# Output projections that open a group get no share of the selection and attention steps in the plan

## The reference

```python
q, k, v, qi, ki, wi, u = mixer_inputs(x, pos, g_pre, w_in)
# per block of 128 queries: index scores, the best 256 keys of each query, attention over these keys
idx = top_k(sum_h(relu(qi_h @ ki.T) * wi_h), 256)
a_o = sparse_attend(q, k[idx], v[idx])
s_o = glu_out(s5_scan(u), w_glu, b_glu)
x   = x + rmsnorm(concatenate([a_o, s_o]) @ w_out)        # output projection
hdn = square(relu(rmsnorm(x) @ w_up))                      # 1024 -> 4096
y   = x + rmsnorm(hdn @ w_down)                            # 4096 -> 1024
```

## Time and profile before

| | us |
|---|---|
| median of 3 runs | 3634.23 (3627.40 to 3640.02) |
| the profiled execution | 3627.5 |
| its span | 3625.8 |
| PE busy in the span | 3036.5 (84%) |
| DVE busy | 1840.4 (51%) |
| ACT busy | 1637.7 (45%) |
| POOL busy | 1262.6 (35%) |

### The profile page before, as it was taken

How to read it: one execution, slowest core, us unless ns; L and a number is a source line. 1 busy time by engine, 2 the same in 40 slices (tenths; PEclk the granted TensorE clock), 3 DMA queues, 4 the chain that set the end, 5 groups by cost and what they waited for, 6 DMA issues and landing times.

```text
span 3625.8 us, 46903 instructions
## 1 busy us (share of the span) xinstructions
PE 3036.5 (84%) x15347; PEld 2396.8 (66%) x15352; DVE 1840.4 (51%) x4116; ACT 1637.7 (45%) x2873; POOL 1262.6 (35%) x1181
## 2 busy tenths in 40 slices
PE   7998545546678889997799999968989999699997
PEld 5887431224556668764577886645778888588885
DVE  4433872862357884468686332666782333511112
ACT  3322413612447755575463555745634554322222
POOL 1333621324013561153265113522672112224444
PEclk9999777877879999998899999988999999899999
DMA  4444344636336564354454223343444213544443
GB/s 149 142 146 142 93 126 133 170 118 202 111 123 232 206 244 134 115 200 154 157 193 169 79 85 124 126 171 122 177 159 136 73 62 131 191 147 150 174 151 125
DMA packets 216109, 529.45 MB, mean 146 GB/s; under 512 B 57514, under 2 KB 110828, under 8 KB 189852
## 3 DMA queue, kind: packets, MB, share of 16 engines
q1 hardware_dynamic: 202924, 501.94, 40.6%
q0 software_dynamic: 11360, 22.60, 2.0%
q10 hardware_dynamic: 1584, 1.90, 0.2%
HBM read 399.43 MB, written 134.12 MB: 147 GB/s over the span
## 4 chain that ended last, share of the span: by engine, by line
PE 50%; DVE 11%; issue 9%; ACT 5%; DMA 4%; POOL 4%; SPq 2%; ACTq 0%; POOLq 0%; DVEq 0%
PE r L1620 16%; PE r L1657 12%; PE po L1708 6%; PE tr L1699 3%; ACT junk_a_b L1982 2%; PE sc L1686 2%; PE sc L1687 2%; POOL acc_b L2124 1%; PE sc L1676 1%; DVE junk_v_b L2363 1%; PE r L1817 1%; POOL hr_b L2105 1%; DVE trial_b L2315 1%; PE tr L1676 1%; PE r L1586 1%
## 5 line engine op out<-in xcount | busy, mean ns | idle before, releaser
L2124 POOL TENSOR_TENSOR acc_b<-acc_b,part_b 128x512 f32<-128x512 f32 x375 | 516.2, 1398 | 483.0 <-ACT part_b L1933 482.1
L1657 PE MATMUL r<-ready_b,h_b 128*128 128x512 f32 x2304 | 574.4, 403 | 41.5 <-ACT part_b L1933 38.3
L1657 PEld LDWEIGHTS r<-ready_b,h_b 128*128 128x128 f32 x2304 | 434.2, 193 | 155.5 <-ACT part_b L1933 51.1
L1620 PE MATMUL r<-x_hi_b,ready_b 128*128 128x512 f32 x1536 | 516.5, 400 | 5.4 <-DVE x_lo_b L2229 2.8
L2105 POOL TENSOR_TENSOR hr_b<-hr_b 128x512 f32<-128x512 f32 x128 | 149.0, 1164 | 766.7 <-ACT hr_b L1920 766.5
L1982 ACT ACTIVATE junk_a_b<-score_b,trial_b 128x384 int8<-128x384 f32 (+13 forms) x266 | 347.4, 1306 | 100.8 <-DVE trial_b L2315 99.7
L1620 PEld LDWEIGHTS r<-x_hi_b,ready_b 128*128 128x128 f32 x1536 | 291.3, 190 | 72.2 <-issue 10.1
L1933 ACT ACTIVATE part_b<-r 128x512 f32<-128x512 f32 x390 | 223.9, 595 | 220.5 <-PE r L1657 131.8
L1708 PEld LDWEIGHTS po<-V_sb,pT_b 128*128 128x128 f32 x2176 | 286.7, 191 | 23.4 <-ACT pT_b L2009 4.5
L1620 PE MATMUL r<-x_lo_b,ready_b 128*128 128x512 f32 x768 | 301.6, 393 | 0.0
L1708 PE MATMUL po<-V_sb,pT_b 128*128 128x64 f32 x2176 | 279.2, 268 | 3.7 <-DVE o_b L2380 3.3
(11 more groups left out here) (407 smaller groups left out, 6061.1 us busy)
## 6 DMA issues: line engine op xcount, KB each, us to landing
ready_b<-ws_u SPq DMA_DIRECT2D x96, 1024.0 KB, 6.6
ready_b<-ws_d SPq DMA_DIRECT2D x96, 1024.0 KB, 5.0
ws_u<-up_b SPq DMA_DIRECT2D x32, 1024.0 KB, 8.7
ws_d<-dn_b SPq DMA_DIRECT2D x30, 1024.0 KB, 6.4
kv_b<-kv_pages POOLq DMA_DIRECT2D x128, 128.0 KB, 3.5
kv_b<-kv_pages SPq DMA_DIRECT2D x128, 128.0 KB, 3.1
raw_b<-w_out SPq DMA_DIRECT2D x64, 256.0 KB, 3.2
raw_b<-w_up SPq DMA_DIRECT2D x32, 512.0 KB, 5.4
```

Of the source, the lines that this page charges most:

```text
L1620: mm = pe.matmul(x[:], wt[:, c], y[:, k], start=k == n == 0, stop=(k, n) == (KD - 1, 2))
L1657: mm = pe.matmul(x[:], f[:, tok], w[:, col], start=c == n == 0, stop=(c, n) == (KQ - 1, 2))
L2124: pool.tensor_tensor(dst, dst, part[:, add_no[key] % 2, :], ALU.add).then_inc(add_pool, 1)
```

## The change

The opening units W(g,0,i) count nothing in the plan, so `merge` puts no side steps behind them, and those steps are dealt over the U and D units. Nothing else is changed; the cost of a unit is read by `merge` alone. Every instruction of both kernels is the same but for what follows from the plan's order.

```diff
     def feed_units(g):
         T = nt(g)
-        out = [(("W", g, 0, i), 5.4) for i in range(T)]
+        out = [(("W", g, 0, i), 0.0) for i in range(T)]
```

## The result

The median went from 3631.35 us (3623.85 to 3640.02, 6 runs) to 3652.41 us (3648.27 to 3656.70, 6 runs): ratio 1.0057, 95% interval 1.0042 to 1.0071. The change makes the kernel 0.57% slower. The forecast was 2.8 us less (3631) and was wrong in its sign: the kernel got 21 us slower. The time lies outside the forecast's own range (3621 to 3645) and inside the wide one (3610 to 3656). The profiled execution took 3651.81 us.

What follows compares the result with a forecast made beforehand. PE, busy 84%, was taken as the bound, with only its holes to gain or lose. Openings -32.5 and moved steps +29.7 gave -2.8 us, so 3634.2 became 3631.4, rounded to 3631; own range 3621 to 3645, wide 3610 to 3656.

Steps and rivals of the forecast that it cites:

- Openings: Openings of groups 0 to 2 without side steps: 17.5, 8.3 and 6.7 us shorter, together -32.5 us.
- S(1,0) and the first of S(1,1) in U(0,0) and U(0,1): Selection steps moved out of group 0's opening: their index matmuls hold PE, costing 7.7 us.
- AB(1)'s cover: Wait for queries at attention's start after group 0: one U replaces four D as cover; cost 0 to 5.5, 3 taken.
- The price of a moved step: Selection stretches: each moved step costs the stretch's mean excess over its feed, 0.77, 0.49 and 0.81 us in groups 0 to 2.
- one choice that costs 5.9: Group 2: all six moved steps belong to one choice; a block beside a choice takes 29.30 us, without 23.40: 5.9 us.
- The rest: 0: Attention, three more D with `beside_search`, and the last attention step one D later: each costs 0.
- one step more in U(1,30) to D(1,15,3): End of group 1: these units get one more selection step, costing 2.3 us.
- DVE bounds group 0: Slower rival: DVE limits group 0's U and D, 15 steps at 3.04 us each; +17.3 us, 3651, chance 0.18.
- a block of 37 us or more beside S(1,2): Group 0's test: such a block, 34.20 us before, at 34 to 35 supports the forecast; 37 or more speaks for DVE.
- The stretch to AB(1): Group 0, from U(0,0): some 297 us if the forecast is right, 316 if DVE binds, 292 if steps hide.
- The port rule: DVE and POOL block each other at a shared SBUF port: ten moved steps lose 2.8 us if DVE is the bound.

Runs made afterwards that it cites:

- e1: Plan of before, with only the opening steps of groups 0, 1 and 2 dealt over their own group's U and D up to AB(g+1): 3651.69 us, 1.0057.
- e4: Plan of before, with only group 2's opening steps dealt over its U and D up to AB(3): 3629.99 us, 0.9994.
- e2: Plan of before, with only group 0's 15 opening steps dealt over its U and D up to AB(1): 3642.20 us, 1.0028.
- e18: The changed kernel with the hidden block's square made by ACT instead of POOL: 3615.83 us, 0.9957 against before.
- e3: Plan of before, with only group 1's 8 opening steps dealt over its U and D up to AB(2): 3645.72 us, 1.0041.
- e14: Plan costs of before, with all side steps 5 cost units (two to three steps) later against the feed: 3646.18 us, 1.0052.
- e5: Kernel of before with each choice's scan and following comparison covering only the first 128 columns, so work is left out: 3612.73 us, 0.9951.
- e13: Plan costs of before, with all side steps 3 cost units (one to two steps) earlier against the feed: 3638.40 us, 1.0017.
- e16: Plan costs of the changed kernel, with all side steps 8 cost units (about four steps) later: 3688.36 us, 1.0160 against before.
- e17: Kernel of before with the hidden block's square made by ACT instead of POOL: 3624.72 us, 0.9977.

## Why the prediction was wrong

- **Openings.** Right: up to U(g,0) they gave 38.2 us, where the sum had 32.5 up to W(g,1,0). Group 0's 26.6 us up to W(0,1,0) came to the tenth, U(0,0) at 1058.2 (about 1060 forecast), and the waits for the third tile's features stayed (11.31 and 8.72 us). The first halves gave 31.1 us of the 32.5 forecast for them; the second halves got 1.8 to 2.8 us shorter in each group, 7.1 in all, which the sum left out.
- **S(1,0) and the first of S(1,1) in U(0,0) and U(0,1).** Forecast 7.7 us, these two units grew by 6.9. Right.
- **AB(1)'s cover.** Bounds 0 to 5.5, value taken 3. PE's timeline shows 12.05 us where the earlier trace rows has 6.10, 5.95 us more: all of the lost cover (5.45) and 0.5 besides. The upper bound was the one to take, since only one U stood between the last selection step and the first attention step.

```profile
1370.49 0.79 PE L1686 MATMUL sc<-KS_sb,qh_b 128*128 128x512 f32 x1 [12.05 <-DMA ql_b<-ql_d]
```

- **The price of a moved step: the step of the sum that failed.** I took the mean excess of a stretch, 0.77, 0.49 and 0.81 us per step, as the price of one step more. But the excess is not made by steps evenly. In the later part of a selection (from U(1,6) and U(2,8) on) blocks without a choice take 21.8 to 24.4 us in before and after with six to eight steps, and one more costs next to nothing; those with three or more steps of a choice take 24.7 to 32.9, by where it falls; those with one or two take anything from 21.8 to 30.1. A denser plan moves every choice of its group against the blocks, and each falls anew. The forecast priced 6.9 + 3.9 us for the moved steps in groups 0 and 1 and 5.9 in group 2, 16.7 in all; the selection stretches took 44.0 less 6.9, 37 us. e1 shows that it is the moved steps that cost this; why they do is shown for U(2,14) alone.
- **Group 2's "one choice that costs 5.9".** It named the right kind of step and the wrong one. The moved choice, S(3,2), ended in U(2,0) to U(2,3) for +0.1 us. S(3,3) and S(3,4), which had not left their stretch but shifted in it, cost 10.2 and 5.4 us more (blocks U(2,6) and U(2,8), and U(2,12) and U(2,14)). In e4, with AB(3) unmoved, the stretch grew by 9.7 and the opening gave 11.6: there the forecast's net for the group was about right.
- **"The rest: 0".** +14.3 us in the stretches behind U(g,16), less the 6 of AB(1). Of this the forecast had 2.3, for one step more in U(1,30) to D(1,15,3), which grew by 3.7. The argument was that engines wait there. It did not ask what the denser steps of the next stage do behind attention: block U(0,26), with nine steps in place of eight, went from 29.7 to 33.5 us, and in group 1 the waits for parts grew by 5.2.
- **The rivals.** "DVE bounds group 0" gave 3651. That it hit the time is luck: it puts the whole loss in group 0, and groups 1 and 2 pay 9.7 and 4.5 us of it. Its test, a block of 37 us or more beside S(1,2), did not come in after (34.7 at most), though one of 37.4 came in e2. The stretch to AB(1) took 298.9 us, where I had said 297 if I am right (the terms add up to 296.1) and 316 if DVE binds. So the step price in group 0 was nearly good by its own test, 17.4 us where 14.6 were forecast. The group as a whole was not: the forecast had some 0 for it, the account has +5.9, and e2, which moves its steps alone, +9.6.
- **The port rule.** The note on the ten steps of S(1,1) sized it at 2.8 us, on DVE's small instructions. The same sharing has its larger effect on the other side: POOL's square takes 4.91 us beside the scan, 1.04 without it, and block U(2,14), 32.9 us in after and 25.3 in e18, shows what hangs on that. The Trainium skill (SBUF — State Buffer, "Who interferes with whom") has the two engines block each other for whole instructions. The row of the square, started 0.07 us behind a scan of 4.15 us and ended 0.83 us behind its end, agrees with it. I read the rule for the mover and not for the one whose turn comes second.

## What to carry to other kernels

The mean excess of a stretch is not the price of one more piece of work in it: look for the blocks that are already free and for those that jump, and ask where the heavy pieces fall after the change. A plan's time can depend on such alignments by as much (15 and 36 us here, at nearly one density) as on what an edit intends (21 us here); a few shifted copies of both plans tell the one from the other. If a plan jumps, follow one jump to its chain: here, an operation between two uses of the in-order engine had been given to an engine that a long instruction can block. With it moved, the loss of 21 us was gone. But one chain explains one block: read the account by stretch again before calling it the cause of the whole.

## What the runs showed of the hardware

- A GpSimd product of 128x512 takes 1.04 us in a block without a choice and 4.91 us when it starts 0.07 us behind a scan of 4.15 us on VectorE; five additions took 13.85 us, 2.77 each, beside the choice (1.29 elsewhere).
- A hole of 3.3 to 3.8 us on TensorE after work at full clock was followed by 8 to 9 us at a granted clock of 0.50 to 0.59 (after's U(2,14) and e3's U(1,10)); in both a second hole, of 4.0 and 3.3 us, lies within these 8 to 9 us. Holes of 1.2 to 1.8 us in before's block U(2,12) left its mean clock at 0.94.
- One kernel's executions scatter more in some plans than in others: e14's from 3635 to 3662 us, e5's from 3611 to 3618. The profiled execution of e14 is the lowest of its own, 11 us below its median, so the block times of e13 to e16 are those of one execution each. Blocks with the same steps repeat well, though: U(2,12) takes 30.4 us in before and in e2. The account by stretches rests on before, after, e17 and e18, whose profiled executions lie within 7 us of their medians.
